# An encoder trunk on one core: the prompt's rows stored in another order, router logits by pass, an exponential ahead of its use, and more dummy transposes

## What is computed

```python
def expert_choice_moe(h, router_w, w_gate, w_up, w_down):      # per request
    cap = EC_CAPACITY * n_tok // N_EXPERTS                     # 2 * n_tok // 16
    aff = jax.nn.softmax((xt @ router_w).astype(F32), axis=-1)
    gates, idx = lax.top_k(aff.T, cap)
    xe = xt[idx]
    hid = jax.nn.silu(xe @ w_gate) * (xe @ w_up)
    ye = (hid @ w_down) * gates[..., None]
    y = jnp.zeros((n_tok, D)).at[idx.reshape(-1)].add(ye)

for i in range(2):
    h = h + mixer_i(rms_norm(h, mix_norm[i]))
    h = h + expert_choice_moe(rms_norm(h, ffn_norm[i]), ...)
    h = h + per_layer_embedding(h, p[i], ...)
return rms_norm(h, final_norm)
```

## Time and profile before

| what | value |
|---|---|
| runs | 2439.77, 2438.33, 2438.50 us; median 2438.5 |
| the profiled execution, span | 2439.0 us; no time of its own around the span is given |
| PE busy | 2353.6 us, 96% of the span |
| DVE, ACT, POOL busy | 1783.9, 1362.2, 299.5 us |
| mean granted clock of PE | 0.983 |
| layer 0's routing and experts | from about 663 to 1249 us |
| layer 1's routing and experts | from about 1740 to 2338 us |

### The profile page before, as it was taken

One profiled execution on the slowest core, in us unless ns is written; L12 is line 12 of the kernel. 1 busy time (PEld: TensorE's weight loads), 2 busy tenths in 40 slices (PEclk: granted clock), 3 DMA queues, 4 the chain that ended last, 5 costly groups with the idle time before them and its releaser, 6 DMA issues.

```text
span 2439.0 us, 34267 instructions
## 1 busy us (share of the span) xinstructions
PE 2353.6 (96%) x12062; PEld 1959.1 (80%) x12062; DVE 1783.9 (73%) x2053; ACT 1362.2 (56%) x1494; POOL 299.5 (12%) x360
## 2 busy tenths in 40 slices
PE   8999999999989999999999999998789999999997
PEld 7888888888768888888878888877578888888876
DVE  7565566465878888888865677765578888888854
ACT  5233233233457777777763555443257777777762
POOL 1000000000111112211111100000111211121011
PEclk9999999999989999999999999998899999999999
DMA  6424333223599999999970534231599999999931
GB/s 236 133 80 137 108 109 126 72 90 103 194 374 395 395 390 389 396 391 393 349 193 17 144 100 112 83 99 61 202 339 388 396 394 390 390 391 394 347 125 43
DMA packets 210973, 577.38 MB, mean 237 GB/s; under 512 B 24384, under 2 KB 65856, under 8 KB 210752
## 3 DMA queue, kind: packets, MB, share of 16 engines
q1 hardware_dynamic: 193584, 526.35, 57.7%
q0 software_dynamic: 17296, 49.83, 8.0%
HBM read 547.80 MB, written 30.43 MB: 237 GB/s over the span
## 4 chain that ended last, share of the span: by engine, by line
PE 90%; DVE 4%; DMA 3%; issue 1%; ACT 1%; POOL 0%; SPq 0%; DVEq 0%; POOLq 0%; ACTq 0%
PE bank L1575 43%; PE bank L1459 40%; PE bank L1396 4%; PE bank L1761 1%; PE bank L1743 1%; DMA rows_normed<-xn_late 1%; DVE d_parts L619 1%; DMA m_x<-rows_normed,idx_t 0%; DMA rows_summed<-m_y,idx_out 0%; DMA resid<-in_x_sample 0%; DMA raw<-in_ret_w_in 0%; ACT d_parts L610 0%; DVE top_i L1988 0%; DMA resid<-rows_summed 0%; DVE m_at L1990 0%
## 5 line engine op out<-in xcount | busy, mean ns | idle before, releaser
L2128 DVE TENSOR_TENSOR w_parts<-wt,w_parts 128x2048 fp32r<-128x2048 f32 x384 | 874.6, 2290 | 135.9 <-ACT w_parts L1157 126.1
L1157 ACT CAST w_parts<-wt 128x2048 fp32r<-128x2048 f32 x384 | 734.3, 1913 | 197.2 <-PE bank L1575 186.3
L1575 PE MATMUL bank<-w_parts,m_xt 128*128 128x512 f32 x2976 | 689.5, 391 | 2.1 <-ACT m_y L1215 2.1
L1575 PEld LDWEIGHTS bank<-w_parts,m_xt 128*128 128x128 f32 x2976 | 556.2, 188 | 117.6 <-issue 2.9
L1459 PE MATMUL bank<-d_parts,xt 128*128 128x512 f32 (+1 forms) x1872 | 383.4, 361 | 4.5 <-DVE d_parts L619 4.4
L1575 PE MATMUL bank<-w_parts,m_hidt 128*128 128x512 f32 x1632 | 384.0, 395 | 2.8 <-DVE m_hidt L2120 2.8
L1459 PEld LDWEIGHTS bank<-d_parts,xt 128*128 128x128 f32 x1872 | 315.9, 190 | 58.4 <-DVE d_parts L619 5.8
L1575 PEld LDWEIGHTS bank<-w_parts,m_hidt 128*128 128x128 f32 x1632 | 306.8, 190 | 66.7 <-issue 3.3
L619 DVE TENSOR_TENSOR d_parts<-raw,d_parts 128x512 fp32r<-128x512 f32 (+1 forms) x168 | 215.6, 1296 | 108.9 <-ACT d_parts L610 108.0
L610 ACT CAST d_parts<-raw 128x512 fp32r<-128x512 f32 (+1 forms) x168 | 183.4, 1107 | 198.9 <-PE bank L1459 195.1
L1459 PE MATMUL bank<-xt,d_parts 128*128 128x256 f32 (+1 forms) x1536 | 284.1, 340 | 5.2 <-DVE d_parts L619 1.9
(11 more groups left out here) (193 smaller groups left out, 2150.4 us busy)
## 6 DMA issues: line engine op xcount, KB each, us to landing
wt<-in_exp_w_gate SPq DMA_DIRECT2D x128, 1024.0 KB, 13.3
wt<-in_exp_w_up SPq DMA_DIRECT2D x128, 1024.0 KB, 12.5
wt<-in_exp_w_down SPq DMA_DIRECT2D x128, 1024.0 KB, 12.7
raw<-in_ret_w_in SPq DMA_DIRECT2D x32, 1024.0 KB, 5.2
raw<-in_na_w_in SPq DMA_DIRECT2D x24, 1024.0 KB, 5.3
raw<-in_ret_w_in SPq DMA_DIRECT2D x32, 512.0 KB, 4.6
raw<-in_ret_w_out SPq DMA_DIRECT2D x16, 1024.0 KB, 5.1
raw<-in_ple_w_gate SPq DMA_DIRECT2D x8, 1024.0 KB, 8.8
```

The source lines that it names most:

```text
L1157: nc.scalar.copy(w_parts[c % RING][:, 0, :], wt[:, place // 2, place % 2 * 2048:place % 2 * 2048 + 2048])\
L1575: last = nc.tensor.matmul(b[:, :], lhs[x][:, 2 * k + j, :], w[:, part, j, f * HALF:(f + 1) * HALF], start=(k == j == 0 and x == part == 0) ...
L2128: v.tensor_tensor(w_parts[c % RING][:, 1, :], wt[:, k // 2, k % 2 * 2048:k % 2 * 2048 + 2048], w_parts[c % RING][:, 0, :].bitcast(F32), AL ...
```

## The change

Five edits, in both layers unless said otherwise.

1. The prompt's residual is no longer stored by POOL ahead of its normed rows. POOL stores the two normed tiles only; SP stores the residual (`store_resid(sp, l, 0)`), on the queue of the weights, after the first gather has landed and ahead of weight chunk 10. `resid_saved` is now one semaphore per group. `rows_stored` waits for the sample's alone. For the prompt's (`resid_stored`) three engines wait: POOL before `gather(1)`, ACT before the first `silu`, DVE before the first `hidden`. `m_x` and `m_hid` swap places, so that the first gather lands over sample tile 2.
2. ACT does one exponential of a constant into `den` before the prompt's squares of layer 0.
3. The prompt's `logits` run by pass: all 8 high by high, all 8 low by high, and only then, after the wait for `xt[1]`, the 8 high by low.
4. Dummies: 36 to 54 and 18 to 40 at the start, 20 to 34 ahead of layer 0's prompt norm, 36 to 46 before the indices, 36 to 54 before the first rows.
5. New dummies: 14 between `logit_tiles` and `affinities`, and in layer 1 16 ahead of each of the prompt's two norm transposes.

```diff
-        m_x = put("m_x", [CAP, D], 144)
+        m_x = put("m_x", [CAP, D], 152)
-        m_hid = put("m_hid", [CAP, D], 152)
+        m_hid = put("m_hid", [CAP, D], 144)
...
+        def resid_stored(eng, l, g):
+
+            eng.wait_ge(resid_saved[l][g], 16 * (len(GROUP_TILES[g]) if l else 1))
...
+        def store_resid(eng, l, g):
+
+            first, n = GROUPS[g]
+            a, z = GROUP_TILES[g][0], GROUP_TILES[g][-1] + 1
+            eng.wait_ge(norm_sq[1 + 3 * l], nth(1 + 3 * l, z - 1))
+            if l:
+                for t in GROUP_TILES[g]:
+                    eng.dma_start(by_tile(rows_summed[l], l, g)[t - a], resid[:, t, :]).then_inc(resid_saved[l][g], 16)
+            else:
+                eng.dma_start(rows_summed[l][first:first + n, :].rearrange("(t p) d -> p t d", p=P),
+                              resid[:, a:z, :]).then_inc(resid_saved[l][g], 16)
...
         def rows_stored(eng, l):
 
-            eng.wait_ge(resid_saved[l], 16 * (TT if l else 2))
+            resid_stored(eng, l, 1)
...
                     if c == 10:
                         sp.wait_ge(moe_rows[l], 16)
+                        store_resid(sp, l, 0)
                     load(c, 0)
...
                 load_gain(3 * l + 3)
+                resid_stored(pool, l, 0)
                 matmuls_done(pool, f"rows{l}", "x1")
                 gather(1)
...
+                    if phase == "first":
+                        resid_stored(act, l, 0)
                     for f in range(2):
                         silu(f)
...
+            act.wait_ge(norm_rs[0], 1)
+            nc.scalar.activation(den[:, 0, 0:1], minus_half[:, 0:1], ACT.Exp)
             for t in range(2):
                 squares(1, t)
...
+                    for wk, xk in ((0, 0), (1, 0), (0, 1)):
+                        if wk == xk == 0:
+                            pe.wait_ge(norm_hi[m], 2 * nth(m, 1))
+                        elif xk:
+                            columns_ready(m, GROUP_TILES[g])
...
                 logit_tiles(l, 0)
+                keep_busy(f"route{l}", "idx", 14)
                 affinities(l, 0)
-                keep_busy(f"route{l}", "gate", 36)
+                keep_busy(f"route{l}", "gate", 46)
...
-                keep_busy(f"rows{l}", "x0", 36)
+                keep_busy(f"rows{l}", "x0", 54)
```

More of the change, by code:

```diff
@@ L520, in build @@
         moe_y_free = [sem(f"moe_y_free{l}") for l in range(2)]
-        resid_saved = [sem(f"resid_saved{l}") for l in range(2)]
+        resid_saved = [[sem(f"resid_saved{l}{g}") for g in range(2)] for l in range(2)]
         resid_in = [sem(f"resid_in{t}") for t in range(TT)]
@@ L675, in tiles_before, with by_tile @@
             return sum(unit(k)[4] for k in range(u))
+        def resid_stored(eng, l, g):
+            eng.wait_ge(resid_saved[l][g], 16 * (len(GROUP_TILES[g]) if l else 1))
+        def by_tile(x, l, g):
+            first, n = GROUPS[g]
+            if l:
+                rows, cols = ((ROWS_P, COLS_P), (ROWS_S, COLS_S))[g]
+                return x[first:first + n, :].rearrange("(r t c) d -> t r c d", r=rows, c=cols)
+            return x[first:first + n, :].rearrange("(t p) d -> t p d", p=P)
+        def store_resid(eng, l, g):
+            first, n = GROUPS[g]
+            a, z = GROUP_TILES[g][0], GROUP_TILES[g][-1] + 1
+            eng.wait_ge(norm_sq[1 + 3 * l], nth(1 + 3 * l, z - 1))
+            if l:
+                for t in GROUP_TILES[g]:
[3 more added lines that the diff above has]
+                              resid[:, a:z, :]).then_inc(resid_saved[l][g], 16)
         def rows_stored(eng, l):
-            eng.wait_ge(resid_saved[l], 16 * (TT if l else 2))
+            resid_stored(eng, l, 1)
             eng.wait_ge(rows_out[l], 16 * 2)
@@ L880, in stored_group @@
             def stored_group(l, g):
-                first, n = GROUPS[g]
-                a, z = GROUP_TILES[g][0], GROUP_TILES[g][-1] + 1
                 done, m = (sample_out if g else rows_out)[l], 1 + 3 * l
-                if l:
-                    rows, cols = ((ROWS_P, COLS_P), (ROWS_S, COLS_S))[g]
-                    by_tile = lambda x: x[first:first + n, :].rearrange("(r t c) d -> t r c d", r=rows, c=cols)
-                    pool.wait_ge(norm_sq[m], nth(m, z - 1))
-                    for t in GROUP_TILES[g]:
-                        pool.dma_start(by_tile(rows_summed[l])[t - a], resid[:, t, :]).then_inc(resid_saved[l], 16)
-                else:
-                    by_tile = lambda x: x[first:first + n, :].rearrange("(t p) d -> t p d", p=P)
-                    pool.wait_ge(norm_sq[m], nth(m, z - 1))
-                    pool.dma_start(rows_summed[l][first:first + n, :].rearrange("(t p) d -> p t d", p=P),
-                                   resid[:, a:z, :]).then_inc(resid_saved[l], 16)
+                if g == 1:
+                    store_resid(pool, l, g)
                 for t in GROUP_TILES[g]:
                     pool.wait_ge(norm_rows[m], nth(m, t))
-                    pool.dma_start(by_tile(rows_normed[l])[t - a], normed(m, t)).then_inc(done, 16)
+                    pool.dma_start(by_tile(rows_normed[l], l, g)[t - GROUP_TILES[g][0]], normed(m, t)).then_inc(done, 16)
             def mixture(l, order):
@@ L1419, in logits @@
             def logits(l, g):
-                columns_ready(1 + 3 * l, GROUP_TILES[g])
+                m = 1 + 3 * l
                 first, n = GROUPS[g]
+                if g == 0:
+                    b, full = fill(pe, route_phase(l, g), ("lg", g))
+                    for wk, xk in ((0, 0), (1, 0), (0, 1)):
[3 more added lines that the diff above has]
+                            columns_ready(m, GROUP_TILES[g])
+                        for j in range(DT):
+                            last = nc.tensor.matmul(b[0:EXPERTS, 0:n], rw_parts[wk][:, l, j, :], xt[xk][:, j, first:first + n],
+                                                    start=(wk == xk == j == 0), stop=(xk == 1 and j == DT - 1))
+                    last.then_inc(full, 1)
+                    return
+                columns_ready(m, GROUP_TILES[g])
                 part_products([rw_parts[k][:, l, :, :] for k in range(2)], lambda k, m, j: xt[k][:, j, first:first + n],
@@ L1486, in queries_keys @@
                            lambda f: slice(f * P, (f + 1) * P), between)
-            keep_busy("ret", ("n0", 0, 0), 36)
+            keep_busy("ret", ("n0", 0, 0), 54)
             norm_columns(0, (0, 1))
-            keep_busy("ret", ("qk", 0, 0), 18)
+            keep_busy("ret", ("qk", 0, 0), 40)
             columns_ready(0, (0, 1))
@@ L1684, in embedding_inputs @@
                                                          for t in range(2)])
-            keep_busy("route0", ("n1", 0, 0), 20)
+            keep_busy("route0", ("n1", 0, 0), 34)
             norm_columns(1, (0, 1))
@@ L1790, in _ @@
                 elif k[:4] == "norm":
+                    if k in ("norm0", "norm1"):
+                        keep_busy("naout", ("n4", int(k[4]), 0), 16)
                     norm_columns(4, (int(k[4]),))
@@ L2144, in mixture @@
                 splits("moe", 0, 0, 1, 2)
+                resid_stored(dve, l, 0)
                 for f in range(2):
```

## The result

The changed kernel takes 2447.91 us (median of 5 runs, 2445.43 to 2449.0), the kernel of before 2438.5. The ratio is 1.003, 95% interval 1.002 to 1.0041, so it is slower, by 5 to 10 us. That is outside the predicted range (2432.8 to 2445.5) and on its slower side; slower had a chance of 0.19.

A forecast was written before the change was run, and what follows sets the result against it. PE, busy 96% of the span, was taken as the bound, so only its waits and low-clock places could be won. Terms -2.5 (layer 0) and +5.3 (layer 1) made +2.8 us: 2441.3 us median, range 2432.8 to 2445.5.

The forecast's parts named there:

- both terms: Up to the second expert's rows: layer 0 gains 2.5 us, layer 1 loses 5.3 us.
- L: Time from SP's first residual store to the landing of all, holding the second gather: 6.3 us layer 0, 13 layer 1.
- Side by side: Layer 1's two residual stores overlap, L = 9.1; sum -2.2, 2436.3 us, same within 0.2%; chance 0.17.
- one behind the other: Layer 1's two residual stores run in sequence on SP's queue, making L = 15.4 us.
- The estimate by the rule of the Trainium skill on the slowest dimension: Layer 1's stores share 4 of 16 engines; 1.05 MB at a quarter of 420 GB/s takes 10 us, L = 12.7.
- the text's own formula: Second rows come 0.1 + L + 0.2 + 8.7 us after the first; layer 1 adds 2.0 us for the clock.
- Storing the normed rows first gives nothing here: Layer 0, first gathered rows: the 3.32 us wait is the gather alone, no store in the chain, so no gain.
- Rival 4: Dummies before the indices run at low clock, 10.6 us against about 6.4; indices 4 us late per layer, +8; chance 0.02.
- The rule on transposes in the Trainium skill: Dummies before the first product: transposes don't count as clock work, so would do nothing for it; the forecast followed the rows instead.
- Rival 3: Layer 1's residual is as slow as on POOL's queue, L = 20.8, deciding from 15.1; +10.6, 2449.1 us; chance 0.12.

The follow-up runs named there:

- the move only: The kernel of before with edit 1 alone, all other edits undone; 2447.54 us, 1.0024 to 1.0052 of before.
- the pieces alone: The changed kernel with layer 1's two prompt residual stores issued by SP as eight stores of 32 rows, all waits kept; 2439.07 us.

## Why the prediction failed

The place, the mechanism and the sign of both terms were right. The step that failed is a size: L, the time until the residual has landed, taken too small in both layers (13 instead of 15.3 us in layer 1, 6.3 instead of 7.9 in layer 0). The other sizes missed by less and to both sides.

**Layer 1's L, the step that failed most.** The step reads "Side by side that makes L = 9.1, one behind the other 15.4 [...] I take 13", and 15.3 was measured. The rows spoke for one behind the other, and the runs show just that; the 13 was a compromise with a case that did not occur. The 15.4 came out right from two wrong parts, though: I had 2.7 us beside the data, as for a quiet load, and 6.35 us a store; measured are 5.1 and 5.1. The estimate by the rule of the Trainium skill on the slowest dimension, 12.7, has the right share of the queue and the same missing time beside the data: 10 us of data and 5.1 make 15.1. With 15.3 the text's own formula gives +7.6 for layer 1 instead of +5.3, the loss measured. In its parts that match is partly luck: the second rows came 24.9 us after the first, 2.9 later than predicted, of which 2.3 are L and 0.7 the gather (9.36 against 8.7); the clock behind the wait cost 1.2 instead of 2.0.

**Layer 0, -1.7 instead of -2.5.** The indices came 2.15 us earlier, as predicted, and the first rows 2.1. Then L of 7.9 instead of 6.3 took 1.6 back; I had priced it between two loads, and this store has 5.4 us beside its 2.5 of data; a second gather of 8.24 instead of 8.7 gave 0.5; the rest is the loop's pace. The first product took 12.74 us in layer 0 and 12.59 in layer 1, where I took 12; the other kernels have 12.5 to 12.9 (three of them 14.0 in layer 0). The 54 dummies did not spare it the clock's fall behind them, but it cost nothing while the second rows came later still.

**"Storing the normed rows first gives nothing here", in layer 0,** was wrong, though the sum contained its worth: I took the 6.1 us of a gather issued at 689 for one issued at 687. Alone the earlier gather took 8.74; only edit 1 made it 6.1.

**The rest.** Layer 1's first rows came 2.4 us earlier (predicted 2.55); the gather went out on the indices, no longer behind a store. The 46 dummies there delayed the indices by 0.1 us, not 0.3: from 1762.40 to 1769.34 it took 6.94 us, with 36 in the run with the move only 6.84. The dummies as such work. Rival 4 is refuted where it was placed: the 46 before the indices took 6.61 us, not 10.6. The rule on transposes in the Trainium skill ("TensorE: Matmul & The Clock Gate", Part 4: PE-mode transpose), that they don't count as work for the clock, disagrees with the start of the kernel, where with 54 and 40 transposes ahead of it the next product took 11.75 us in nine of nine executions, and with 36 and 18 in two of five. ACT's and DVE's new waits and the weights behind the stores cost nothing in the changed kernel, because PE's own delay covered them; take it away and the weights cost 3.0 us.

**The sum.** By the measured terms it is +7.6 - 1.7, about +6, and the ratio's interval (4.9 to 10) holds that. Added to the 2438.5 of before it is 2444.4, so the forecast, with every size put right, would still have stayed in its range and below the 2447.9 measured. The median has 3.5 us more than the terms. Taking edit 1 back removes all of it (2438.89), so it comes with edit 1; but single executions go 2 to 3 us up or down by the clock, there is one profile of each kernel, and where that rest lies stays open. Rival 3 was priced at L from 15.1 to 20.8 with a chance of 0.12, and 15.3 lies at its near end. My own sum for one behind the other was 15.4 and the rows spoke for it, so far more than 0.12 belonged there.

## What to carry to other kernels

Before a wait is placed, ask what the waiting instruction really needs. POOL's second gather needed nothing of the residual, only the first scatter did; moving one line of wait brought 7 us. Count a store's landing as its data plus the time that stores showed beside it, from a store's row and not from a load's, and look at its outermost dimension: two stores of 4 pieces of 32 rows ran at a quarter of the rate and landed after 15.3 us, the same rows as eight stores after 8.5, issuing included. And an operand that is ready earlier is worth something only if the transfer that it starts meets a quiet queue.

## What the runs showed of the hardware

- A DMA store from SP took some 5 us beyond its data until its semaphore was seen (estimates: 10.2 less 5.1; 7.9 less 2.5), a load 2.7. Not all of it need be fixed: the same 1 MB store of layer 0 landed after 7.8 to 9.6 us in the kernels that have it ahead of the last chunks, slowest where the second gather runs beside it. In the kernel with the pieces alone a store of 128 KB took 3.8 to 4.5 us.
- Two stores in the shape 4x32x1024 from one queue do not overlap (10.2 and 15.3 us), the second at about 103 GB/s. In the shape 2x32x1024 they held the DMA engines at 51 to 53 GB/s, a share of 0.13, while two loads of 1 MB issued from 1780.98 on stood behind them.
- A gather of 96 rows took 6.1 us where the DMA engines fell quiet some 2 us after its issue, 8.74 where they moved about 400 GB/s until 5 us after it.
- The kernel of before itself ran between 2435.8 and 2444.7 us over the later runs, wider than the 1.4 us of its first ones. When the high clock comes back in the 24 matmuls at 39.7, behind 4.4 to 4.7 us in which PE idles, differs between executions of like code: between 42 and 43 in one (7.17 us for the product), after 45 in another (8.53).
